# Branch order, group-norm tail, token range of layer 1 and expert boundary of a two-layer trunk, rearranged

## What is computed

```python
mean = jnp.mean(y, axis=-1, keepdims=True)                 # y: output of the recurrence, per head
var = jnp.mean(jnp.square(y - mean), axis=-1, keepdims=True)
y = ((y - mean) * lax.rsqrt(var + RWKV_GN_EPS)).reshape(B, L, RWKV_WIDTH) * ln_g + ln_b
y = (y + bonus.reshape(B, L, RWKV_WIDTH)) * g              # branch B is ready here
...
ga, gb, gc = jnp.split(jax.nn.sigmoid(pg), N_BRANCH, axis=-1)   # pg: gate columns of xn @ w_in
merged = ga * (ya @ w_proj_a[i]) + gb * (yb @ w_proj_b[i]) + gc * (yc @ w_proj_c[i])
h = h + merged @ w_out[i]
hn = rms_norm(h, norm_ffn[i])
...
y = y + gates[..., e:e + 1] * swiglu(x, wg[e], wu[e], wd[e])    # experts, layer 1
return rms_norm(h, norm_final)[:, N_META:]
```

## Time and profile before

| | before |
|---|---|
| median of 3 runs | 2392.31 us (2390.92 to 2393.53) |
| profiled execution | 2395.66 us, its span 2392.7 us |
| PE busy | 2181.8 us, 91% of the span |
| DVE, ACT busy | 1398.5 us (58%), 1196.7 us (50%) |
| mean DMA rate | 202 GB/s, in the experts 313 to 377 GB/s |

### The profile page before, as it was taken

The page is one execution under the profiler, slowest core; times in us unless marked ns, Lnnn a source line. Parts: engine busy times, 40 slices in busy tenths (PEclk is TensorE's granted clock), DMA queues, the critical chain, the costliest instruction groups (busy, mean ns, idle before and its releaser), DMA issues.

```text
span 2392.7 us, 35192 instructions
## 1 busy us (share of the span) xinstructions
PE 2181.8 (91%) x14894; PEld 1850.8 (77%) x14894; DVE 1398.5 (58%) x1206; ACT 1196.7 (50%) x1116; POOL 22.3 (1%) x24
## 2 busy tenths in 40 slices
PE   7998985969999899998597799999999999999996
PEld 4757685969999675768597688888888787888885
DVE  2512336454444342133544688888888888888884
ACT  2134244323333123524432577777777777777673
POOL 0000010000000000001000000000000000000000
PEclk9998998979999899999898799999999999999998
DMA  5222101424444122110142498989898898989891
GB/s 184 111 66 108 71 3 71 177 82 184 168 176 161 71 106 88 71 71 3 53 171 95 168 370 316 371 321 364 336 357 351 338 367 314 373 317 376 322 371 76
DMA packets 73545, 484.38 MB, mean 202 GB/s; under 512 B 12392, under 2 KB 13544, under 8 KB 15704
## 3 DMA queue, kind: packets, MB, share of 16 engines
q1 hardware_dynamic: 69672, 478.62, 51.8%
q10 hardware_dynamic: 3760, 4.09, 0.6%
HBM read 480.94 MB, written 1.74 MB: 202 GB/s over the span
## 4 chain that ended last, share of the span: by engine, by line
PE 85%; DVE 8%; ACT 3%; issue 2%; DMA 1%; DVEq 0%; ACTq 0%; SPq 0%
PE PS L440 19%; PE PS L442 18%; PE PS L441 18%; PE PS L521 5%; PE PS L758 5%; PE PS L686 3%; DVE area L1456 3%; PE PS L493 2%; PE PS L633 2%; DVE WL L1456 2%; PE PS L607 2%; PE PS L647 1%; PE PS L482 1%; PE PS L965 1%; PE PS L1024 1%
## 5 line engine op out<-in xcount | busy, mean ns | idle before, releaser
L1456 DVE TENSOR_TENSOR WL<-ring,WH 128x2048 fp32r<-128x2048 f32 x414 | 944.1, 2290 | 333.5 <-ACT WH L1093 195.6
L1389 ACT ACTIVATE WH<-ring 128x2048 fp32r<-128x2048 f32 x336 | 643.3, 1916 | 189.5 <-PE PS L442 144.9
L440 PE MATMUL PS<-WH,XGH 128*128 128x512 f32 x896 | 356.1, 397 | 14.3 <-DVE WL L1456 11.0
L442 PE MATMUL PS<-WL,XGH 128*128 128x512 f32 x896 | 349.8, 390 | 0.0
L441 PE MATMUL PS<-WH,XGL 128*128 128x512 f32 x896 | 349.3, 390 | 0.0
L1093 ACT ACTIVATE WH<-ring 128x2048 fp32r<-128x2048 f32 x78 | 148.9, 1910 | 164.3 <-PE PS L442 164.3
L440 PEld LDWEIGHTS PS<-WH,XGH 128*128 128x128 f32 x896 | 168.3, 188 | 52.6 <-DVE WL L1456 15.9
L442 PE MATMUL PS<-XL,WH 128*128 128x272 f32 x704 | 204.2, 290 | 0.0
L442 PEld LDWEIGHTS PS<-WL,XGH 128*128 128x128 f32 x896 | 168.2, 188 | 36.0
L441 PEld LDWEIGHTS PS<-WH,XGL 128*128 128x128 f32 x896 | 168.4, 188 | 33.3
L440 PE MATMUL PS<-WH,HTH 128*128 128x512 f32 x448 | 176.7, 394 | 0.7 <-DVE WL L1456 0.2
(11 more groups left out here) (290 smaller groups left out, 3217.5 us busy)
## 6 DMA issues: line engine op xcount, KB each, us to landing
ring<-in_experts SPq DMA_DIRECT2D x336, 1024.0 KB, 6.9
ring<-in_weights SPq DMA_DIRECT2D x114, 1024.0 KB, 6.8
ring<-in_weights SPq DMA_DIRECT2D x4, 576.0 KB, 6.1
ring<-in_weights SPq DMA_DIRECT2D x4, 512.0 KB, 4.0
cst<-in_consts ACTq DMA_DIRECT2D x1, 1316.0 KB, 7.5
area<-in_x ACTq DMA_DIRECT2D x2, 512.0 KB, 4.4
out<-area SPq DMA_DIRECT2D x2, 512.0 KB, 2.6
bias_line<-lin SPq DMA_DIRECT2D x1, 672.0 KB
```

The costliest lines, as they stand in the source:

```text
L440: pe.matmul(o, lh, rh, start=first, stop=False, skip_group_check=True)
L442: return pe.matmul(o, lh, rl, start=False, stop=last, skip_group_check=True)
L1389: act.activation(WH[(BASE + j) % 3][:, :], ring[b][:, 2048 * (j % 2):2048 * (j % 2) + 2048], ACT.Copy).then_inc(S("w_hi"), 1)
L1456: tt = lambda o, a_, b_, op: dve.tensor_tensor(o, a_, b_, op)
```

## The change

The diff does four things.

- **Order of the branches.** `MERGE_ORDER = (0, 2, 1)`: branch C's gates and projection come ahead of branch B's, so the stage runs P0, G20, G21, P2, G10, G11, P1, O0, O1, and SP loads in that order.
- **The group-norm tail** moves into the merge stage. The stage end between them is gone; yA's high part, the first conversions and P0 come among the steps of the norm. The reciprocal is cut into four quarters (`spread`), the rest into `scaled` and `normed`, all hooked behind halves of G20 and G21. ACT's copy of branch C waits for P0 to finish (the two share a buffer, `YH0`), that of branch B for `n_y`.
- **Token range.** `FIRST = (0, META)`: in layer 1 the early gates, gates, projections and output product work on columns 16 to 271, 256 of the 272. Sums and sigmoids of the stage follow. The product with `SG` is written over `SG`, a fourth buffer `TMP` and a small memset are gone.
- **Expert boundary.** `AHEAD = 4`: h3 of the next expert is converted, too, before DVE waits for the scatter. The selection matrices are made later, behind h10 (`select_rows`) and h22 (`select_tokens`).

```diff
+MERGE_ORDER = (0, 2, 1)
...
-        for b in range(3):
+        for b in MERGE_ORDER:
...
-        (_, MG, SG, TMP) = carve(area2, [(4, TP), (KT, T), (KT, T), (4, T)])
+        (_, MG, SG) = carve(area2, [(KT, T), (KT, T), (KT, T)])
+        (GN,) = carve(area2[:, 9 * 4 * TP:], [(4, T)])
+        FIRST = (0, META)
...
+        AHEAD = 4
...
+                        ins = three_products(PS[:, bank0 + dt, lo:T], wh[:, c], wl[:, c], xh(k), xl(k), k == 0, k == KT - 1)
...
-                        ins = pe.matmul(PS[:, 5 + n % 3, 0:T], early_bufs[0][:, k, (n % 4) * P:(n % 4 + 1) * P], xn[:, k, 1:T + 1],
+                        ins = pe.matmul(PS[:, 5 + n % 3, lo:T], early_bufs[0][:, k, (n % 4) * P:(n % 4 + 1) * P], xn[:, k, 1 + lo:T + 1],
...
+                    ins = pe.matmul(PS[:, 4 + p, 0:T], C("headones"), GN[:, p, :], start=True, stop=True)
                 ins.then_inc(S("n_v"), 1)
-                end_stage(pe, "pe")
-                for b in range(3):
+                for j, b in enumerate(MERGE_ORDER):
...
+                    pe.wait_ge(S("x_lo"), 7 * l + (1, 4, 5)[j])
                     y_lo = [YL[0], YL[1][:, :, PADC:TP], YL[2]][b]
                     for half in range(2):
                         def before(d_):
-                            if b and half == 0 and d_ % 4 == 0:
-                                pe.wait_ge(S("m_s"), at("m_s", l, 2 * b + d_ // 4))
-                        rows_half(l, f"P{b}", half, lambda k: YH[b][:, k, :], lambda k: y_lo[:, k, :], half == 0, half == 1, before,
+                            if j == 0 and half == 0 and d_ == 4:
+                                pe.wait_ge(S("n_e"), at("n_e", l, 0))
+                            if j and half == 0 and d_ % 4 == 0:
+                                pe.wait_ge(S("m_s"), at("m_s", l, 2 * j + d_ // 4))
+                        rows_half(l, f"P{b}", half, lo, lambda k: YH[b][:, k, lo:], lambda k: y_lo[:, k, lo:], half == 0, half == 1, before,
...
+                act.activation(YH[0][:, :, :], yA[:, :, :], ACT.Copy).then_inc(S("x_hi"), 1)
+                high_half(first_split[l])
                 act.wait_ge(S("n_d"), at("n_d", l, 0))
-                act.activation(K[:, :, PADC:TP], Y[:, :, PADC:TP], ACT.Square).then_inc(S("n_sq"), 1)
-                high_half(first_split[l])
+                act.activation(GN[:, :, :], Y[:, :, PADC:TP], ACT.Square).then_inc(S("n_sq"), 1)
+                high_half(first_split[l] + 1)
                 act.wait_ge(S("n_e"), at("n_e", l, 0))
-                act.activation(K[:, :, PADC:TP], K[:, :, PADC:TP], ACT.Sqrt).then_inc(S("n_s"), 1)
-                high_half(first_split[l] + 1)
-                end_stage(act, "act")
-                act.activation(YH[0][:, :, :], yA[:, :, :], ACT.Copy).then_inc(S("x_hi"), 1)
+                act.activation(GN[:, :, :], GN[:, :, :], ACT.Sqrt).then_inc(S("n_s"), 1)
                 for h in range(2):
-                    act.activation(SG[:, 4 * h:4 * h + 4, :], EG[:, 4 * h:4 * h + 4, :], ACT.Sigmoid).then_inc(S("m_s"), 1)
+                    act.activation(SG[:, 4 * h:4 * h + 4, lo:], EG[:, 4 * h:4 * h + 4, lo:], ACT.Sigmoid).then_inc(S("m_s"), 1)
                 act.wait_ge(S("m_s"), at("m_s", l, 1))
                 high_half(first_split[l] + 2)
                 act.activation(XH[:, 0:4, :], xn[:, 0:4, 1:T + 1], ACT.Copy).then_inc(S("x_hi"), 1)
                 act.activation(XH[:, 4:8, :], xn[:, 4:8, 1:T + 1], ACT.Copy).then_inc(S("x_hi"), 1)
-                for b, y in ((1, R[:, :, PADC:TP]), (2, yC[:, :, :])):
+                def branch_high(j):
+                    b = MERGE_ORDER[j]
+                    if j == 1:
+                        act.wait_ge(S("w_used"), split_half[(l, f"P{MERGE_ORDER[0]}")] + 2)
+                    else:
+                        act.wait_ge(S("n_y"), l + 1)
+                    y = {1: Y[:, :, PADC:TP], 2: yC[:, :, :]}[b]
                     act.activation(YH[b][:, :, :], y, ACT.Copy).then_inc(S("x_hi"), 1)
-                def gates(b, h):
-                    act.wait_ge(S("w_used"), split_half[(l, f"G{b}{h}")] + 2)
-                    if b:
-                        act.wait_ge(S("m_read"), at("m_read", l, 2 * (b - 1) + h))
-                    act.activation(SG[:, 4 * h:4 * h + 4, :], PS[:, 4 * h:4 * h + 4, 0:T], ACT.Sigmoid).then_inc(S("m_s"), 1)
+                def gates(j, h):
+                    act.wait_ge(S("w_used"), split_half[(l, f"G{MERGE_ORDER[j]}{h}")] + 2)
+                    if j == 1:
+                        act.wait_ge(S("m_read"), at("m_read", l, h))
+                    else:
+                        act.wait_ge(S("m_free"), at("m_free", l, h))
+                    act.activation(SG[:, 4 * h:4 * h + 4, lo:], PS[:, 4 * h:4 * h + 4, lo:T], ACT.Sigmoid).then_inc(S("m_s"), 1)
...
                 def merged_high(h):
+                    act.wait_ge(S("m_free"), at("m_free", l, 2 + h))
+                    act.activation(XH[:, 4 * h:4 * h + 4, lo:], MG[:, 4 * h:4 * h + 4, lo:], ACT.Copy).then_inc(S("x_hi"), 1)
                 events = {}
-                for b in range(1, 3):
+                after_half(events, l, f"P{MERGE_ORDER[0]}", 1).append((branch_high, 1))
+                for j in range(1, 3):
                     for h in range(2):
-                        after_half(events, l, f"G{b}{h}", 1).append((gates, b, h))
+                        after_half(events, l, f"G{MERGE_ORDER[j]}{h}", 1).append((gates, j, h))
...
+                after_half(events, l, f"P{MERGE_ORDER[1]}", 0).append((branch_high, 2))
                 for h in range(2):
-                    after_half(events, l, "P2", 1).append((merged_high, h))
+                    after_half(events, l, f"P{MERGE_ORDER[2]}", 1).append((merged_high, h))
...
                 for j in range(3, HALVES):
-                    expert_high(n, j)
+                    if j >= AHEAD:
+                        expert_high(n, j)
                     for do, f in events.get(j, []):
...
-                    expert_high(n + 1, 2)
+                    for j in range(2, AHEAD):
+                        expert_high(n + 1, j)
...
-                v(dve.reciprocal(K[:, :, TR], K[:, :, TR]))
-                v(tt(Y[:, :, TR], Y[:, :, TR], K[:, :, TR], ALU.mult))
-                for p in range(4):
-                    ins = dve.tensor_scalar(Y[:, p, TR], Y[:, p, TR], prm_col(l, "ln_g", p), prm_col(l, "ln_b", p), ALU.mult, ALU.add)
-                v(ins)
-                v(tt(Y[:, :, TR], Y[:, :, TR], BN[:, :, TR], ALU.add))
-                v(tt(R[:, :, TR], Y[:, :, TR], GT[:, :, TR], ALU.mult))
-                end_stage(dve, "dve")
...
+                def spread(p):
+                    ins = dve.reciprocal(GN[:, p, :], GN[:, p, :])
+                    if p == 3:
+                        v(ins)
+                def scaled():
+                    v(tt(Y[:, :, TR], Y[:, :, TR], GN[:, :, :], ALU.mult))
+                    for p in range(4):
+                        ins = dve.tensor_scalar(Y[:, p, TR], Y[:, p, TR], prm_col(l, "ln_g", p), prm_col(l, "ln_b", p), ALU.mult, ALU.add)
+                    v(ins)
+                def normed():
+                    v(tt(Y[:, :, TR], Y[:, :, TR], BN[:, :, TR], ALU.add))
+                    tt(Y[:, :, TR], Y[:, :, TR], GT[:, :, TR], ALU.mult).then_inc(S("n_y"), 1)
+                dve.wait_ge(S("n_m"), at("n_m", l, 0))
+                dve.scalar_tensor_tensor(Y[:, :, TR], PS[:, 0:4, 0:T], -1.0 / HD, Y[:, :, TR], ALU.mult, ALU.add).then_inc(S("n_d"), 1)
                 low_half(first_split[l])
+                dve.wait_ge(S("n_v"), at("n_v", l, 0))
+                dve.tensor_scalar(GN[:, :, :], PS[:, 4:8, 0:T], 1.0 / HD, GN_EPS, ALU.mult, ALU.add).then_inc(S("n_e"), 1)
+                operand_low(1, YL[0][:, :, :], yA[:, :, :], YH[0][:, :, :])
                 low_half(first_split[l] + 1)
-                operand_low(1, YL[0][:, :, :], yA[:, :, :], YH[0][:, :, :])
                 low_half(first_split[l] + 2)
                 for i in range(2):
                     q = slice(4 * i, 4 * i + 4)
                     operand_low(2 + i, XL[:, q, 1:T + 1], xn[:, q, 1:T + 1], XH[:, q, :])
-                operand_low(4, YL[1][:, :, TR], R[:, :, TR], YH[1][:, :, :])
-                operand_low(5, YL[2][:, :, :], yC[:, :, :], YH[2][:, :, :])
-                def gated(b, h):
+                dve.wait_ge(S("n_s"), at("n_s", l, 0))
+                spread(0)
...
+                    if j == 0:
+                        tt(MG[:, q, lo:], SG[:, q, lo:], PS[:, q, lo:T], ALU.mult).then_inc(S("m_read"), 1)
+                    else:
+                        tt(SG[:, q, lo:], SG[:, q, lo:], PS[:, q, lo:T], ALU.mult).then_inc(S("m_read"), 1)
+                        dve.wait_ge(S("m_read"), at("m_read", l, 2 * j + h))
+                        if j == 2:
+                            dve.wait_ge(S("m_free"), at("m_free", l, h))
+                        tt(MG[:, q, lo:], MG[:, q, lo:], SG[:, q, lo:], ALU.add).then_inc(S("m_free"), 1)
...
```

(35 more changed lines are left out.)

76 lines of the change are left out of this document (36 added, 40 removed).

## The result

| | before | after |
|---|---|---|
| median (range, runs) | 2392.66 us (2390.92 to 2393.53, 4) | 2334.74 us (2332.60 to 2339.77, 4) |
| profiled execution, its span | 2395.66, 2392.7 us | 2339.77, 2338.0 us |
| ratio of the medians, 95% interval | | 0.9762 [0.9745, 0.9779] |

What follows compares the result with a forecast made beforehand. PE was taken to bound the kernel, with 85% of the chain. Savings of 33.8 + 5.2 + 2.0 + 12.1 = 53.1 us from 2392.3 gave 2339 us, 2.2% faster; range 2330 to 2352.

Steps and rivals of the forecast that it cites:

- The head: Start of the merge stage in both layers: G20 starts earlier, saving 16.9 us a layer, 33.8 us in both.
- The new wait: Merge stage, ahead of G20: PE waits 3.2 us for DVE's product with the gate.
- The rival of an overbooked DVE: Merge stage: pieces meant to hide hold a weight half, the head gives 14 us a layer, 2345 us; chance 0.11.
- 256 columns: Layer 1's merge stage: 16 halves with 768 matmuls, each 6.7 ns shorter for 16 fewer columns, saving 5.2 us.
- The weight-load rival: Layer 1's merge stage: weight load sets the matmul distance at 272 columns, so 5.2 us becomes 0, 2344 us; chance 0.08.
- the narrow-matmul rival: Layer 1: narrow matmuls shed more, at the scatter product's rate, 10.0 us for 5.2 and 3.2 for 2.0, 2333 us; chance 0.11.
- The early gates: Layer 1's eight early gates, 16 records each: fewer columns save 0.25 us each, 2.0 us, bounds 0 and 3.2.
- The last rival: Merge stage: 256 columns run like the plain form, 0.217 us a matmul, making the kernel slower, 2423 us; chance 0.02.
- The boundary between experts: Experts: PE's waits for h3's low part at seven boundaries go, saving 12.1 us.
- The rival that transfers take the gain: Experts: a shorter boundary gives weight transfers less time to get ahead; all 12.1 us gone, 2351 us; chance 0.13.
- my picture of one queue that needs both edits: Expert boundary, DVE's queue: h3's low part follows h2's, ready by 1603.4 where PE wants 1606.4; selections behind h10 cost 0.
- the sum with the skill's slope: Layer 1's columns by the Trainium skill's 0.13 ns a column: the term would be 1.6 us, the whole sum 49.6.

## Why the prediction was right, point by point

**The head: 16.9 us a layer forecast, 16.4 in layer 0, and 17.1 in layer 1** (22.8 less the columns' 5.7). The walk with the old durations in the new order put P0 at 4.8 and G20 at 19.9 us behind the second head sum; in layer 1 they came at 4.68 and 19.74. In layer 0 they came at 6.11 and 21.35, as the sum took 1.4 us longer at the lower clock level; the forecast had no such term. That 16.4 still came out there is partly luck: O0 had 3.4 us at the lower level in place of 5.6 before, which gave 1.1 us back. Its main claim, that DVE's queue (fed by ACT's third high part, as reckoned) and not P0 sets G20's start, was tested twice: with a quarter of the reciprocal taken out of the way G20 came 1.7 us sooner behind P0, and with P0 1.6 us faster it came at the same time.

**The new wait was forecast at 3.2 us and is 1.4 and 1.9.** The step that failed is P0's length. I took two halves at the rate of the earlier trace rows, 12.1 us. P0 ran 3.4 us at the lower clock level and took 13.1 us in layer 1, with fewer columns. The sum did not notice, since the wait absorbs it. In the kernel before the same slow start was on the path, and the way I counted from G10's end included it unseen.

**Nothing else became late in the stage.** The pieces of the norm's tail, the waits of ACT and the loads stayed hidden, as reckoned; no wait for WL or for branch B's low part. The rival of an overbooked DVE fell.

**256 columns: 5.2 forecast, 5.7 measured** (16 halves by 0.355 us). The slope between 272 and 512 columns was somewhat too flat: from 272 to 256 the cost fell in proportion to the columns, 0.1258 to 0.1184 us, 7.4 ns for 16. The weight-load rival (nothing gained) and the narrow-matmul rival (13 ns) both fell at 256. The early gates gave 0.22 us each, 1.8 for 2.0.

**The last rival, slower because a narrower matmul runs at another price,** did not come at 256. With 128 columns the stage costs 71 us more than with 256, but not by the price: at the lower clock level both cost the same, 0.213 and 0.214 us. There the clock stayed at that level, which the rival did not speak of.

**The boundary between experts: 12.1 forecast, 14.9 measured.** This is the term that was mis-sized. A regular distance went from 127.2 to 125.3, 1.9 us where I had 1.73 as a mean over the seven. At a boundary before, the two distances between matmuls around the wait are 2.05 and 0.34 us where 0.227 each is usual, 1.93 us too much; the forecast counted the first and not the second. Three of the seven distances before were 0.5 us longer still, for waits inside the expert (0.5 to 0.6 us of PE's weight load for DVE's low part) that followed late transfers; those went, too, though the changed kernel run again has one such wait, in its last distance. The rival that transfers take the gain had the sign wrong: with the fourth half ACT's waits for them were shorter in all ten profiles. The single parts explain the rest: the moved selections alone give 10.7 us over the seven distances, the fourth half alone 13.0, so my picture of one queue that needs both edits was too strict.

**The total:** 33.8 + 5.2 + 2.0 + 12.1 forecast; 33.5 + 5.7 + 1.8 + 14.9 = 55.9 measured by stages. The spans differ by 54.7 and the medians by 57.9; what the clock grants in the untouched stretches moves a run by several microseconds either way. That the total fell within a few microseconds of the forecast is so partly by luck. A slip of the forecast: by its own terms the sum with the skill's slope is 49.5 us, not 49.6; nothing hangs on it.

## What to carry to other kernels

Where an engine idles in a tail of small steps, walk the other engines' queues through the new order with the old durations before moving work there: the engine that holds the next stage, and by how much, could be read to 0.2 us where the clock was what it had been before, and was 1.4 us off where it was not. Then look at the granted clock behind each wait that is left: a wait of 3.4 us ahead of O0 cost another 1.7 to 2.6 us in the slow matmuls behind it (half of 3.4 and of 5.3 us), and idle matmuls in the wait bought that back. When columns are cut, measure the distance of the new width before relying on it. And compare two kernels that differ by less than some 10 us stage by stage, with the granted clock beside it, as five runs of one kernel here lay between 2320.6 and 2336.7 us.

## What the runs showed of the hardware

- After waits of PE of 2.6 and 3.5 us, ahead of the second head sum, P0 and O0, the granted clock was often, though not always, at its lower level for some 3.4 to 5.3 us (0.214 us for 0.118 from matmul to matmul at 256 columns). Twelve constant matmuls (2.88 us) in the wait ahead of O0 kept it at 1.0 there. The kernel with them is 14 to 16 us faster by the ratios (0.9695 against 0.9762 and 0.9754), more than the 5 to 7 us of the merge stages themselves; that the rest comes from the filling is not shown, and a run with fillings did not have it.
- Stretches with equal work differ by up to 8 us between kernels, and between runs of one kernel by some microseconds (346 to 354 us in layer 1 ahead of its head sum), along with the time at the lower level in them (21 to 41 us).
- Fast float32 matmuls with a weight load each cost 0.227 us at 512 columns, 0.126 at 272, 0.118 at 256, at full clock, and at half clock 0.227 at 272 (P0 of the kernel before), 0.214 at 256 and 0.213 at 128; at 128 the clock stayed at its lower level for 170 us of work without a pause, in the one run made.
